# Mixers A and C of an encoder kernel issued in rounds of two pairs, with a sixth probability slot

## The reference

```
h = x @ w_in                              # one projection, columns split among three mixers
oa = window_attn(a_q, a_k, a_v, sink, t5) # A: 8 heads, +-128 tokens, one extra "sink" logit per head
ob = mla(...)                             # B: 4 heads, dense over all positions
oc = neighborhood_attn(c_q, c_k, c_v, rpb)# C: 4 heads, 8x16 neighbourhood on a 64-wide grid
o  = concat(oa*silu(a_g), ob*silu(b_g), oc*silu(c_g)) @ w_out
x  = layer_norm(alpha * x + o)
```

## Time and profile before

| | |
|---|---|
| median of 3 runs | 1842.55 us (1841.69 to 1842.91) |
| the profiled execution | 1846.45 us, of which the span is 1844.7 us |
| busy in the span | PE 97%, PEld 80%, DVE 51%, ACT 42%, POOL 23% |
| mean granted clock of PE | 0.997 of full speed |
| chain that ended last | PE 91%, DVE 6%, ACT 1%, issue 1%, DMA 1% |
| of it by line | L633 66%, L758 8%, L728 8%, L710 6% |

### The profile page before, as it was taken

The page is one execution under the profiler, slowest core; times in us unless marked ns, Lnnn a source line. Parts: engine busy times, 40 slices in busy tenths (PEclk is TensorE's granted clock), DMA queues, the critical chain, the costliest instruction groups (busy, mean ns, idle before and its releaser), DMA issues.

```text
span 1844.7 us, 32212 instructions
## 1 busy us (share of the span) xinstructions
PE 1798.5 (97%) x12530; PEld 1467.1 (80%) x12530; DVE 945.6 (51%) x2060; ACT 772.2 (42%) x1666; POOL 431.5 (23%) x668
## 2 busy tenths in 40 slices
PE   4999999999999999999999999999999999999997
PEld 4887689889987666889989866988898766578897
DVE  6365765211425776555463476550133277565638
ACT  2345754211125666553233366441212366755510
POOL 0353402311111273001162223140111224600010
PEclk9999999999999999999999999999999999999999
DMA  6676332211124122004145552521212061200022
GB/s 232 174 248 173 107 126 92 92 46 47 47 69 124 27 65 80 1 1 149 35 155 160 155 139 70 183 92 37 67 47 69 23 149 40 95 12 2 24 81 92
DMA packets 148308, 167.16 MB, mean 91 GB/s; under 512 B 18320, under 2 KB 134416, under 8 KB 147648
## 3 DMA queue, kind: packets, MB, share of 16 engines
q1 hardware_dynamic: 145792, 157.64, 28.6%
q0 software_dynamic: 1152, 4.19, 0.6%
q10 hardware_dynamic: 1216, 3.28, 0.5%
HBM read 143.00 MB, written 32.65 MB: 95 GB/s over the span
## 4 chain that ended last, share of the span: by engine, by line
PE 91%; DVE 6%; ACT 1%; issue 1%; DMA 1%; POOL 0%; SPq 0%; DVEq 0%
PE psum L633 66%; PE psum L758 8%; PE psum L728 8%; PE psum L710 6%; DVE nmax L1147 2%; PE psum L769 1%; DVE pt_sb L1178 1%; PE psum L643 1%; DMA w_stage<-w_in 1%; PE psum L615 0%; POOL gT L1405 0%; DVE w_lo L517 0%; PE psum L596 0%; ACT w_stage L898 0%; DVE x_lo L1138 0%
## 5 line engine op out<-in xcount | busy, mean ns | idle before, releaser
L633 PE MATMUL psum<-w_hi,x_hi 128*128 128x256 f32 (+1 forms) x1344 | 380.9, 283 | 3.3 <-DVE x_lo L1138 3.3
L633 PE MATMUL psum<-w_hi,x_lo 128*128 128x256 f32 (+1 forms) x1344 | 379.2, 282 | 0.0
L633 PE MATMUL psum<-w_lo,x_hi 128*128 128x256 f32 (+1 forms) x1344 | 376.8, 280 | 0.0
L633 PE MATMUL psum<-x_hi,w_hi 128*128 128x512 f32 x816 | 325.5, 399 | 0.5 <-POOL w_lo L517 0.5
L633 PE MATMUL psum<-x_lo,w_hi 128*128 128x512 f32 x816 | 324.4, 398 | 0.0
L633 PE MATMUL psum<-x_hi,w_lo 128*128 128x512 f32 x816 | 324.4, 398 | 0.0
L517 POOL TENSOR_TENSOR w_lo<-w_stage,w_hi 128x1024 fp32r<-128x1024 f32 (+1 forms) x79 | 159.2, 2023 | 685.9 <-ACT w_hi L929 685.8
L517 DVE TENSOR_TENSOR w_lo<-w_stage,w_hi 128x1024 fp32r<-128x1024 f32 (+1 forms) x81 | 139.1, 1734 | 298.9 <-ACT w_hi L929 298.9
L633 PEld LDWEIGHTS psum<-w_hi,x_hi 128*128 128x128 f32 x1344 | 254.3, 189 | 3.9 <-DVE x_lo L1138 3.7
L633 PEld LDWEIGHTS psum<-w_lo,x_hi 128*128 128x128 f32 x1344 | 256.4, 191 | 0.2
L633 PEld LDWEIGHTS psum<-w_hi,x_lo 128*128 128x128 f32 x1344 | 253.5, 189 | 0.0
(11 more groups left out here) (148 smaller groups left out, 2602.2 us busy)
## 6 DMA issues: line engine op xcount, KB each, us to landing
w_stage<-w_in SPq DMA_DIRECT2D x48, 512.0 KB, 4.4
w_stage<-w_in SPq DMA_DIRECT2D x88, 256.0 KB, 3.4
toep<-rpb_tile SPq DMA_DIRECT2D x12, 1152.0 KB, 15.5
rpb_tile<-rpb_col SPq DMA_DIRECT2D x48, 192.0 KB
hT<-y SPq DMA_DIRECT2D x18, 512.0 KB, 5.5
y<-hT SPq DMA_DIRECT2D x18, 512.0 KB, 2.7
w_stage<-w_out SPq DMA_DIRECT2D x32, 256.0 KB, 4.1
w_stage<-w_out SPq DMA_DIRECT2D x16, 512.0 KB, 5.3
```

What stands on the lines that cost most here:

```text
L633: last = nc.tensor.matmul(out, w, x, start=(n == 0 and part != 1), stop=(n == len(pairs) - 1 and part != 0))
```

## The change

PE's order in phase AC becomes rounds of a group: four scores (of group g), the transposes of the last pair of group g-1, both value steps of group g-1, its R, and then the transposes of the first pair of group g. ACT and DVE get loops over pairs in place of those over units: first the two exponentials (or bounds) of pair p, then the copies of pair p-1, with `group_rinv` and `group_scale` between them on DVE and `group_out` behind them. A sixth probability slot, `pAC_last`, is a tensor of its own; it overlies a buffer of the gates, so POOL's sink column of unit 5 waits for the last gate. Mixer B keeps its order.

```diff
+    if ph == "AC":
+        for g in range(n // 2 + 1):
+            if g < n // 2:
+                steps += [("S", i) for i in range(4 * g, 4 * g + 4)]
+            if g:
+                steps += [("T", 2 * g - 1, 0), ("V", 2 * g - 2), ("V", 2 * g - 1), ("R", g - 1)]
+            if g < n // 2:
+                steps.append(("T", 2 * g, 0))
+        return steps
...
-P_SLOTS = 5
+P_SLOTS = 6
...
+                pAC_last = sb("pAC_last", [P, 385], F32, st2)
...
+        def p_slot(i):
+            return pAC[:, i % P_SLOTS, :] if i % P_SLOTS < 5 else pAC_last[:, :]
...
+                    for p in range(len(U) // 2 + 1 if ph == "AC" else 0):
+                        for i in range(max(2 * p, EARLY), min(2 * p + 2, len(U))):
+                            exp_unit(s, i, U[i])
+                        for i in range(max(2 * p - 2, 0), 2 * p):
+                            pt_copy(s, U[i], 0)
...
+                    for p in range(len(U) // 2 + 2 if ph == "AC" else 0):
+                        for i in range(max(2 * p, EARLY), min(2 * p + 2, len(U))):
+                            bound_scores(s, i, U[i])
+                        g = p // 2 - 1
+                        if p % 2 == 0 and g >= 0:
+                            group_rinv(s, ph, g)
+                        elif g >= 0:
+                            group_scale(s, ph, g)
+                        for i in range(max(2 * p - 2, 0), min(2 * p, len(U))):
+                            pt_copy(s, U[i], 0)
+                        if p % 2 and g >= 0:
+                            group_out(s, ph, g)
...
+                    if i == P_SLOTS - 1:
+                        pool.wait_ge(silu_done, last_gate(s))
```

More of the change, by code:

```diff
@@ L220, in pe_steps @@
             steps.append(("S", 2 * j))
-            if ph != "B":
-                steps.append(("S", 2 * j + 1))
         if 0 <= j - 1 < n:
@@ L226, in pe_steps @@
             steps.append(("R", (j - late) // 2 - 1))
-        if j < n and ph == "B":
+        if j < n:
             steps.append(("S", 2 * j + 1))
@@ L338, in encoder_kernel @@
         kB_lo = [w[:, 1].rearrange("p k n -> p (k n)").rearrange("p (h n) -> p h n", h=2) for w in (w_hi, w_lo)]
-        pAC = w_stage[:, :, :, :].rearrange("p h k n -> p (h k n)")[:, 0:P_SLOTS * 385].rearrange("p (u n) -> p u n", n=385)
+        pAC = w_stage[:, :, :, :].rearrange("p h k n -> p (h k n)")[:, 0:5 * 385].rearrange("p (u n) -> p u n", n=385)
+        def p_slot(i):
+            return pAC[:, i % P_SLOTS, :] if i % P_SLOTS < 5 else pAC_last[:, :]
         t5_neg = hflat[0:A_HEADS, 5 * DM:5 * DM + 512]
@@ L721, in transpose_probs @@
                     pe.wait_ge(probs_done, probs_no[s, u])
-                    src = pB[:, i % 3, :] if ph == "B" else pAC[:, i % P_SLOTS, :]
+                    src = pB[:, i % 3, :] if ph == "B" else p_slot(i)
                     ps = wait_free(pe, ("PT", s, u, hf))
@@ L897, in exp_unit @@
                         act.wait_ge(sink_put, sink_no[s, u])
-                    nc.scalar.activation(pAC[:, i % P_SLOTS, 0:m], pAC[:, i % P_SLOTS, 0:m], ACT.Exp, bias=nmax[:, j:j + 1],
+                    nc.scalar.activation(p_slot(i)[:, 0:m], p_slot(i)[:, 0:m], ACT.Exp, bias=nmax[:, j:j + 1],
                                          scale=-1.0, accum_out=psums[:, j:j + 1]).then_inc(probs_done, 1)
@@ L1033, in _ @@
                                                  ACT.Copy).then_inc(b_hi_done, 1)
-                    for i in range(len(U) + LAG_T):
+                    for p in range(len(U) // 2 + 1 if ph == "AC" else 0):
[3 more added lines that the diff above has]
+                            pt_copy(s, U[i], 0)
+                    for i in range(len(U) + LAG_T if ph == "B" else 0):
                         if 0 <= i - LAG_T < len(U):
@@ L1040, in _ @@
                                 pt_copy(s, U[i - LAG_T], 0)
-                        if (EARLY if ph == "AC" else 0) <= i < len(U):
+                        if i < len(U):
                             exp_unit(s, i, U[i])
-                        if ph == "B" and i == len(U) - 3:
+                        if i == len(U) - 3:
                             out_high(s, 0)
@@ L1157, in bound_scores @@
                         dve.wait_ge(biasA_loaded[t - 1], 16 * (s + 1))
-                    nc.vector.tensor_tensor_reduce(out=pAC[:, i % P_SLOTS, 0:n], in0=ps[:, 0:n], in1=reversed_keys(biasA[:, t - 1, kv, :] if t else biasA0[:, kv, :], k0, n),
+                    nc.vector.tensor_tensor_reduce(out=p_slot(i)[:, 0:n], in0=ps[:, 0:n], in1=reversed_keys(biasA[:, t - 1, kv, :] if t else biasA0[:, kv, :], k0, n),
                                                    scale=1.0, scalar=nsink[:, A_HEADS * (s // 2) + h:A_HEADS * (s // 2) + h + 1], op0=ALU.add, op1=ALU.min,
@@ L1162, in bound_scores @@
                     dve.wait_ge(biasC_done, biasC_no[s, u])
-                    nc.vector.tensor_tensor_reduce(out=pAC[:, i % P_SLOTS, 0:n], in0=ps[:, 0:n], in1=biasC[:, i % 3, 0:n],
+                    nc.vector.tensor_tensor_reduce(out=p_slot(i)[:, 0:n], in0=ps[:, 0:n], in1=biasC[:, i % 3, 0:n],
                                                    scale=1.0, scalar=3e38, op0=ALU.add, op1=ALU.min,
@@ L1334, in _ @@
                                                     qB_hi[0:BD, :, q_tile(t)].bitcast(F32), ALU.subtract).then_inc(free(key), 1)
+                    for p in range(len(U) // 2 + 2 if ph == "AC" else 0):
[10 more added lines that the diff above has]
+                            group_out(s, ph, g)
                     lag = 8 if dense_wide(ph, s) else 10
-                    for i in range(len(U) + lag - 2):
-                        if (EARLY if ph == "AC" else 0) <= i < len(U):
+                    for i in range(len(U) + lag - 2 if ph == "B" else 0):
+                        if i < len(U):
                             bound_scores(s, i, U[i])
@@ L1456, in sink_column @@
                     n, h = key_tiles(U[i], s) * P, A_HEADS * (s // 2) + 4 * kv + t
+                    if i == P_SLOTS - 1:
+                        pool.wait_ge(silu_done, last_gate(s))
                     if i >= P_SLOTS:
                         wait_full(pool, ("PT", s, U[i - P_SLOTS], 0))
-                    nc.gpsimd.tensor_copy(pAC[:, i % P_SLOTS, n:n + 1], nsink[:, h:h + 1]).then_inc(sink_put, 1)
+                    nc.gpsimd.tensor_copy(p_slot(i)[:, n:n + 1], nsink[:, h:h + 1]).then_inc(sink_put, 1)
                 def window_bias(i):
```

## The result

The changed kernel takes 1853.73 us (median of 4 executions, 1851.44 to 1855.58), the kernel before 1842.41 (4 executions, 1841.69 to 1842.91). The ratio is 1.0055, with a 95% interval of 1.0043 to 1.0067: slower by more than 0.2%, as forecast. The profiled executions are 1855.57 and 1846.45 us, 9.1 apart.

The account below looks back on a forecast made before the run. PE's list bounds phase AC; its 26 us saving would be lost to a loop through DVE and ACT. Per-run losses of 2.4 and 1.6, twice both, gave +8.0, less 0.3 for ends: 1850.2 us, range 1843.5 to 1858.

Parts of the forecast that it names:

- what PE's list saves: PE in phase AC: fewer block changes save 0.36 us a group, 26 us over 72 groups, if PE never waits.
- rival 1: At the value step: ACT's copy is in time and PE runs its list, 1816.5 us; chance 0.06.
- the loop: Phase AC: value steps wait for ACT's copy, behind exponentials, behind DVE's out and bound; +8.0 us in all.
- the low price of the wait, 0.05: PE's wait for ACT's copy ahead of the value step costs 0.04 to 0.05 us, not 0.15.
- rival 3: Phase AC: waits at the high price, or both copies late, 1855 to 1858 us; chance 0.08.
- the ends of the phase: First and last groups of a phase wait for one copy or spread as before; 0.3 us taken off.
- the scale of the final number: Whole kernel: 1854.1 us profiled and 1850.2 median, the profiled execution before lying 3.9 above its median.
- Rival 2: No change: the loop's legs overlap by 0.1 us more than read, 1843 to 1844 us; chance 0.12.
- Rival 4: PE's short idles in each round drop its clock to 1.2 GHz, 94 us more; chance 0.02.

Follow-up runs that it names:

- experiment 6: Experiment 1 with a group's spread sums (R) put between a pair's transposes and the value steps, DVE's scale and out a group later: 1821.42 us, ratio 0.9881.
- experiment 7: Edits of experiment 5 and experiment 6 together, so R moved and DVE's wait named first: 1820.57 us, ratio 0.9879.
- Experiment 1: Changed kernel with ACT's copy of the previous pair placed between the two exponentials, not behind both: 1831.23 us, ratio 0.9928.
- experiment 4: Changed kernel with DVE's scale moved from ahead of the first pair's copy to behind it: 1878.13 us, ratio 1.0183.
- experiment 3: Changed kernel with five probability slots instead of six, and without POOL's wait for the gate: 1852.13 us, ratio 1.0041.
- Experiment 8: Changed kernel with PE's value steps naming the wait for DVE's copy first, ACT's second: 1860.16 us (median of 3), ratio 1.0084.
- experiment 2: Kernel before with only PE's new order of steps; ACT and DVE loops and five slots unchanged: 1833.14 us, ratio 0.9943.
- experiment 5: Experiment 1 with PE's value steps in mixers A and C naming the wait for DVE's copy first, ACT's second: 1826.87 us, ratio 0.9906.

## Why the prediction was right, step by step

**Right: what PE's list saves.** 0.36 us per group. Experiments 6 and 7 run the list without a stall and give 3.48 to 3.50 and 4.78 in mixer C against 3.47 and 4.77 forecast. Over the whole phase they save 21 and 22 us of the 26: the ends of the phase are not rounds, and in mixer A something is left to wait for (two groups of run 0 take 8.42 and 8.37 us, where the list alone would take 9.01 - 0.72 = 8.29). The block prices stayed what the earlier trace rows gave. The Trainium skill, TensorEngine Tiling (Array Packing), under Tiling Modes, says that a change of tiling mode drains the engine. The trace agrees that a change costs time: with fewer changes the C group of run 0 takes 3.48 to 3.50 us in place of 3.83. The rule says nothing of who is late next, and that decided against rival 1.

**Right: the loop.** Forecast and measured R to R: 4.05 and 4.04 (C, run 0), 5.11 and 5.11 (C, run 1), 5.16 and 5.17 (A, 384 keys), 9.40 and 9.41 (two groups of A, run 0), 19.72 and 19.76 (four, run 1). The wait named for it was the one that the waits view shows. Experiment 1 opens the loop on ACT and the stall goes; experiment 4 lengthens it on DVE and the time follows; experiment 3 takes the slots away and nothing happens.

**Right: the low price of the wait, 0.05.** In the round shown above PE starts 0.05 behind ACT's copy. Experiment 8 shows what rival 3 would have been: 352.68 - 346.76 = 5.9 us more.

**Off: the ends of the phase.** This is the term that was mis-sized: "I take 0.3 off for them". The gaps from R to R are as forecast, but for a run's last two and for the one or two in which mixer A gives way to C, which had no sum of their own. Without the last two they sum before and after to 38.74 and 40.72 in run 0 (nine gaps), 103.37 and 105.07 in run 1 (21 gaps), +1.98 and +1.70. What lies outside them (from the first transpose to the first R, the last two gaps, from the last R to mixer B) is 12.24 and 12.85 in run 0, 14.25 and 14.74 in run 1: +0.61 and +0.49. Over four runs that makes +7.35 and +2.2, together the 9.55 seen, where the prediction had +8.0 (over 72 groups; these are only 60 gaps) and -0.3. The last round shows why. It has no scores to cover the copies, and the timeline after has two waits of PE in it:

```profile
216.90 0.38 ACT L917 ACTIVATE pt_sb<-psum 128x256 f32<-128x256 f32 x1 [0.28 <-PE psum L740]
...
217.43 0.41 PE L740 MATMUL psum<-ident,w_stage 128*128 128x128 f32 x2 [0.34 <-ACT pt_sb L917]
...
218.03 1.34 PE L770 MATMUL psum<-pt_sb,vwin 128*64 128x128 f32 x16
218.14 0.42 DVE L1195 COPY pt_sb<-psum 128x256 f32<-128x256 f32 x1 [0.18 <-PE psum L740]
...
219.30 0.44 PE L781 MATMUL psum<-ident,rinv_wide 128*128 128x128 f32 x2
```

The transposes wait for ACT's copy; the two value steps, one block of 1.34, contain a wait for DVE's copy (the same 16 records would be busy for 1.12, as the kernel before has them at its own end). The last R comes 3.09 after the one ahead. Before, the last two gaps were 5.07 together, and now they are 7.13; the earlier first R (5.45 after the first transpose in place of 6.90) makes that good only in part.

**Off: the scale of the final number.** The profiled sum was 1854.1 against 1855.57 measured; the phases account for it, with +9.55 in place of +7.7. The median forecast, 1850.2, is 3.5 below the one measured, of which the phases are 1.9. The rest is in no round: two of the four executions of the changed kernel are at 1851.4 to 1851.9, two at 1855.6, and the four of the kernel before all at 1841.7 to 1842.9. So the medians compare a mixed set with an unmixed one, and their distance of 11.3 us overstates the change: the two lower executions lie 9.3 above the median before, and the profiled executions, both of the higher kind, 9.1 apart. The last section tells of a stretch that goes with it.

**The rivals.** Rival 1 fell as worked out: ACT's copy is not in time, and experiment 1 shows the gain where it is. Rival 2 fell: no leg overlaps more than was read. Rival 4 fell: PE stalls for about 0.3 to 0.6 us in nearly every round of 4 to 5 us, through 120 us of run 1, and the clock stays at 1.00, its level of 2.4 GHz (the window of 569 to 700 us after: PE busy 124.91 of 131.00, clock 1.00). The Trainium skill, TensorE: Matmul & The Clock Gate, under A second HAM failure mode, tells of short idles between groups of matmuls that bring the clock down, in a bf16 kernel. The idles here, in a 32-bit one, did not.

**Not foreseen, but not needed: DVE's copy.** It is hidden in the changed kernel behind the longer stall. Once that stall goes, it costs 0.17 us per round (experiments 1 and 2), 0.08 to 0.09 of it through the order of two waits (experiment 5), the rest through its nearness to the transposes (experiment 6). My expectations of experiments 1 and 2 had priced it at next to nothing, and were 5 to 9 us too low for that.

## What to carry to other kernels

When a reordering gathers PE's work into fewer and longer blocks, write down the loop that now runs from the last operation of a block through every other engine and back, in the order in which those engines take their work; the gain is real only as far as that loop is shorter than PE's list. Here PE's order alone gained 9 us, and the loops of ACT and DVE that came with it cost 19. Putting the copy that PE wants first ahead of one exponential, and one short step of PE between a transpose and the product that needs its copy, gave 21 of PE's 26 us, and 22 with the order of the waits changed too. The rounds at either end of a phase need a sum of their own: they have no cover.

## What the runs showed of the hardware that was not expected

**The order of two waits.** A value step waits for two copies. With the late one named first in the code, PE starts about 0.05 us behind the copy; named second, the same wait costs 0.09 to 0.10 us more in each round. Over the four phases that is 5.9 us in experiment 8, and in experiment 5, the same effect the other way, 4.2 us.

**A stretch at half clock near the start, in some executions.** Windows of the kernel before (us; busy of PE, PEld, DVE, ACT, POOL; clock; DMA share; GB/s):

```profile
40.00:43.30 3.30, 1.60 (x11) 1.09 (x11) 1.88 (x3) 0.00 (x0) 0.59 (x1) 1.00 0.98 338
43.30:46.80 3.50, 3.50 (x8) 2.04 (x7) 0.90 (x3) 1.15 (x2) 0.28 (x1) 0.50 0.99 279
46.80:50.10 3.30, 3.30 (x9) 2.53 (x9) 1.30 (x2) 1.15 (x2) 2.25 (x2) 0.50 0.78 308
50.10:53.50 3.40, 3.40 (x16) 2.76 (x15) 1.74 (x6) 1.83 (x3) 0.00 (x0) 0.99 0.97 253
```

The same windows of experiment 1:

```profile
40.00:43.30 3.30, 1.60 (x8) 0.57 (x7) 1.62 (x3) 0.00 (x0) 0.00 (x0) 1.00 1.00 318
43.30:46.80 3.50, 3.50 (x16) 2.81 (x17) 0.83 (x3) 1.15 (x2) 0.78 (x1) 1.00 1.01 298
46.80:50.10 3.30, 3.30 (x16) 2.66 (x15) 1.49 (x3) 1.15 (x2) 1.78 (x2) 1.00 0.63 237
```

In both, PE had been idle for half of the 3.3 us before. In the one it then ran at 0.50, its level of 1.2 GHz, for 6.8 us, and issued about half as many matmuls; in the other it didn't. The edits lie behind this point, so PE has the same work up to here, but not at the same moments: from 36 to 40 us it was busy for 2.33 us in the one and for 2.62 in the other. The first scores of run 0 start at 159.29 us in the one and at 155.51 in the other, 3.8 us apart; 6.8 us at half the clock make 3.4 of that. The profiles of the kernel before and after both have this stretch, those of all eight experiments don't. That fits the whole times, which fall into two groups some 4 us apart (in the last set the kernel before gives 1846.0 to 1846.2 four times and 1842.2 to 1842.3 three times); for executions that were not profiled it is inferred, not shown. It is why the length of a phase in the trace tells these kernels apart better than the median of four. Whether the different moments from 36 to 40 us decide it or something else stays open.
